# Loading the key and value weights inside the retention, and attention's tables inside the projection, in a one-core Trainium2 decoder layer

## The chip, the core and the metric

The kernel is one launch on one core of a Trainium2 chip. The metric is the device time of that launch in microseconds (us), the median of several executions. The engines are TensorE (PE in the rows; PEld is its weight load), VectorE (DVE), ScalarE (ACT), GpSimd (POOL) and SyncE (SP), which here only issues DMAs. Each engine works through its own queue in order. They meet in semaphores, and at the end of each block of the program in a barrier of all five.

## What is computed

One layer of a decoder trunk on 1088 tokens (1024 of a prompt, 64 of eight sampled sequences), width 1024, in float32. A feed-forward half step and a norm stand ahead of a mixer, and one more of each behind it. The change touches only the mixer:

```python
rq, rk, rv, rg, sq, sk, sv = project_in(x, w_in)        # retention q, k, v, gate; attention q, k, v
o_ret = retention(rq, rk, rv, state)                    # 8 heads x 64, chunks of 128 tokens
y_ret = silu(rg) * (o_ret - mean) * rsqrt(var + eps) * gn_w     # per head: the group norm
o_swa = sliding_window_attention(sq, sk, sv, bias, sinks)       # 8 query heads, 2 key/value heads
merged = concat([y_ret, o_swa]);  m = merged @ w_out
```

## The kernel before

A float32 product is made of three passes (L108): each operand is split into a rounded high part and a low part, and high x high, high x low, low x high are added up in PSUM. For weights the split is a ScalarE copy (`round_tile`, raw to `w_hi`) and a GpSimd subtraction (`split_tile`, raw minus `w_hi` to `w_lo`), and only then can TensorE use the tile.

**The order of the stages.** One block holds the first feed-forward step, the retention's projection and the retention (L1988 on). Two more blocks follow, one for the group norm with attention's projection, one for attention (L2043 to L2048); then a block for the output projection and the second feed-forward step.

**The end of the retention.** `retention_stage` goes through nine token tiles (eight of 128, the last of 64 sampled tokens). After the last one TensorE makes four more products for the sampled sequences' states (L1183), with two PSUM banks. VectorE folds each into `state_dec` (L1229), and when the fourth is folded SyncE issues the store of `state_dec` (L1089). The two stores of the prompt's state (L1087) were issued earlier. `outputs_stored` counts all three stores.

**Group norm and projection.** `group_norm_and_projection_stage` has six weight tiles (first keys and values, then four of queries) and three chunks of tokens for each, so 18 steps j of `project` (24 matmuls each, bank by bank). The group norm's nine token tiles u run between them. TensorE turns a tile of retention output to rows (`turn`, L1302); VectorE centres it (`centre`, L1352 to L1356); ScalarE squares it (L1403); VectorE sums the squares (L1362), ScalarE takes the root (`deviation`, L1408), VectorE the reciprocal (L1364, together `invert`); GpSimd multiplies (`normalise`, L1449); TensorE turns it back (`back`, L1312); VectorE multiplies by gain and gate (`gate`, L1373); ScalarE rounds this to `mix_hi` (`high`, L1421); GpSimd subtracts for `mix_lo` (`low`, L1455). TensorE's order is turn(0), turn(1), then for every j: project(j), turn(j+2), back(j-1). VectorE's is, for every u: centre(u), invert(u-1), gate(u-2). `gate` writes one of two `mixed` buffers, so from the third tile on it waits for `low` of the tile two before it (`lo_done`). ScalarE and GpSimd follow the loops of L1426 and L1463. The two slots of `stage` take the raw weights; SyncE waits for `room`, the three stores of the retention, ahead of its first load (L1290).

**Attention.** SyncE issues the two halves of the bias table, the sampled tokens' bias, the key and value caches and eight tiles of `w_out`, then the stores (L1557 on). TensorE makes scores for a block of 128 queries as a pair of key/value heads (`score_pair`, L1603, two pairs of score banks, of which the second pair is requested only after the first has been read: `biased`); VectorE scales them and adds the bias (L1675), which needs the scores and the table.

Of the kernel before, what the change touches and what calls it, by code (L numbers as in the profile page):

```python
# [63 lines left out]
class Stage:  # L64
# [5 lines left out]
    def __init__(self, sync=None, scalar=None, gpsimd=None, tensor=None, vector=None, sync_early=None,  # L70
# [5 lines left out]
                 added=None, sync_second=None):  # L76
# [9 lines left out]
        self.added, self.sync_second = added, sync_second  # L86

# [943 lines left out]
def retention_stage(core, at, tables_at, tables_room, ready, tables, g_chunk, g_dec, state_in, q_t, k_t, k_tok, v_tok, state_out,  # L1031
# [21 lines left out]
    q_dec = [m.put(f"{tag}q_dec{i}", [P, PAIRS, P]) for i in range(2)]  # L1053
    probs = [m.put(f"{tag}probs{i}", [P, 2, PAIRS * P]) for i in range(2)]
# [20 lines left out]
    def sync(sp):  # L1075
# [170 lines left out]
    return Stage(sync=sync, gpsimd=gpsimd, tensor=tensor, vector=vector, scalar=scalar, outputs_stored=(stored, 48))  # L1246


def group_norm_and_projection_stage(core, at, at_small, eps, gn_w, o_t, gate_t, mix_hi, mix_lo, w_in, xh, xl, ident,
                                    q_t, k_t, v_tok, room):  # L1250
# [13 lines left out]
    mixed = [m.put(f"{tag}mixed{u}", [P, PAIRS, P]) for u in range(2)]  # L1264
    m = Layout(core.nc, at)
    rows = [m.put(f"{tag}rows{u}", [P, HEADS, HD]) for u in range(3)]
    squares = m.put(tag + "squares", [P, HEADS, HD])
    stats = [m.put(f"{tag}stats{u}", [P, 5, HEADS]) for u in range(3)]
    w_hi = [m.put(f"{tag}w_hi{n}", [P, D_MODEL], F32R) for n in range(2)]
    w_lo = [m.put(f"{tag}w_lo{n}", [P, D_MODEL], F32R) for n in range(2)]  # L1270
# [17 lines left out]

    def sync(sp):
# [100 lines left out]

    def scalar(act):
        def round_tile(n):
            act.wait_ge(staged[n % 2], 16 * (n // 2) + 16)
            if n >= 2:
                act.wait_ge(proj_done, N * (n - 1))
            act.activation(w_hi[n % 2][:, :], stage[:, n % 2, :], ACT.Copy).then_inc(w_hi_done, 1)

# [20 lines left out]
        def high(u):  # L1418
            a, b = tile_tokens(u)
            act.wait_ge(gated, u + 1)  # L1420
# [822 lines left out]
```

## Time and profile before

| | us |
|---|---|
| median of 3 runs | 2205.27 |
| lowest, highest | 2204.52, 2205.83 |
| the profiled execution | 2202.61 |
| its span in the trace | 2200.8 |

| stretch of the profiled span | from, to (us) |
|---|---|
| end of the retention's block, group norm with projection | about 1052 to 1171 |
| attention | about 1171 to 1262 |
| everything ahead and behind | 0 to 1052, 1262 to 2201 |

All times in the rows count from the start of the span. A row of a timeline merges equal instructions that follow each other: the first number is the start of the first, the second the time from there to the end of the last. What stands in square brackets is how long the engine had been idle before it and who ended the wait. PEclk is the clock that TensorE was granted, as a share of 2.4 GHz.

### The profile page before, as it was taken

What the parts mean: (1) busy time and instruction counts of PE and PEld (TensorE: products, weight loads), DVE (VectorE), ACT (ScalarE), POOL (GpSimd) and SP (SyncE); (2) the same over time, 40 slices, a digit from 0 to 9 for tenths busy, and PEclk for the clock granted to TensorE, in tenths of its full rate; (3) what the DMA queues carried; (4) which work ended last, traced back from release to release, by engine and by line L of the source; (5) the groups of instructions that cost most, each with busy time, mean ns of one, the idle gap of its engine ahead of it and who ended that gap; (6) DMA issues with size and microseconds to landing.
All of it is one profiled execution on the core that took longest, in us unless ns stands there. A gap on an engine that the chain in (4) does not pass through costs nothing. (4 is left out here: it accounts for less than half of the span.)

```text
span 2200.8 us, 31129 instructions
## 1 busy us (share of the span) xinstructions
PE 2111.7 (96%) x11989; PEld 1937.3 (88%) x11989; DVE 910.0 (41%) x1690; ACT 507.0 (23%) x887; POOL 518.4 (24%) x257
## 2 busy tenths in 40 slices
PE   8999999999999989999786799899999999999997
PEld 8999999999999979998685478899999999999996
DVE  5534343443534360004434823434434343535346
ACT  4121211111111252111134722311111111121215
POOL 4221212122121231223142412221221212121213
PEclk9999999999999999999798999999999999999999
DMA  7111010101011021101104030101010101111012
GB/s 279 35 52 57 29 57 29 57 29 57 29 57 47 30 91 42 46 29 42 60 20 144 1 120 1 58 29 58 29 57 29 57 29 57 40 46 57 29 58 82
DMA packets 38058, 118.40 MB, mean 54 GB/s; under 512 B 6255, under 2 KB 10863, under 8 KB 37743
## 3 DMA queue, kind: packets, MB, share of 16 engines
q1 hardware_dynamic: 37999, 117.58, 15.0%
q8 instruction: 41, 0.67, 0.1%
q14 instruction: 18, 0.15, 0.0%
HBM read 106.29 MB, written 11.27 MB: 53 GB/s over the span
## 5 line engine op out<-in xcount | busy, mean ns | idle before, releaser
L111 PE MATMUL bank<-x_hi,f_w_hi 128*128 128x362 f32 (+1 forms) x2104 | 688.8, 327 | 7.5 <-issue 5.6
L113 PE MATMUL bank<-x_hi,f_w_low 128*128 128x362 f32 (+1 forms) x2104 | 690.3, 328 | 0.0
L355 POOL TENSOR_TENSOR f_w_low<-f_w_raw,f_w_hi 128x1024 fp32r<-128x1024 f32 x132 | 317.3, 2420 | 1179.3 <-ACT f_w_hi L285 1179.3
L543 DVE TENSOR_TENSOR acc<-bank,acc 128x512 f32<-128x512 f32 x720 | 467.1, 688 | 8.2 <-PE bank L441 5.8
L521 DVE TENSOR_TENSOR f_h_full<-bank,f_silu 128x362 f32<-128x362 f32 (+1 forms) x132 | 70.7, 535 | 818.2 <-PE bank L113 815.9
L111 PEld LDWEIGHTS bank<-x_hi,f_w_hi 128*128 128x128 f32 x2104 | 396.7, 189 | 9.6 <-issue 7.8
L113 PEld LDWEIGHTS bank<-x_hi,f_w_low 128*128 128x128 f32 x2104 | 396.4, 188 | 0.0
L112 PE MATMUL bank<-x_lo,f_w_hi 128*128 128x362 f32 (+1 forms) x1056 | 345.8, 327 | 0.0
L112 PE MATMUL bank<-x_low,f_w_hi 128*128 128x362 f32 (+1 forms) x1048 | 342.9, 327 | 0.0
L439 PE MATMUL bank<-f_w_hi,f_h_hi 128*128 128x512 f32 x640 | 250.8, 392 | 0.0
L441 PE MATMUL bank<-f_w_low,f_h_hi 128*128 128x512 f32 x640 | 250.1, 391 | 0.0
L440 PE MATMUL bank<-f_w_hi,f_h_lo 128*128 128x512 f32 x640 | 249.9, 390 | 0.0
L294 ACT ACTIVATE f_silu<-bank 128x362 f32<-128x362 f32 (+1 forms) x132 | 62.5, 474 | 683.7 <-PE bank L113 683.7
L112 PEld LDWEIGHTS bank<-x_lo,f_w_hi 128*128 128x128 f32 x1056 | 199.2, 189 | 0.9
L112 PEld LDWEIGHTS bank<-x_low,f_w_hi 128*128 128x128 f32 x1048 | 197.2, 188 | 0.8
L300 ACT ACTIVATE f_h_hi<-f_h_full 128x362 fp32r<-128x362 f32 (+1 forms) x132 | 67.0, 508 | 529.0 <-DVE f_h_full L521 529.0
L441 PEld LDWEIGHTS bank<-f_w_low,f_h_hi 128*128 128x128 f32 x640 | 120.1, 188 | 26.7
L439 PEld LDWEIGHTS bank<-f_w_hi,f_h_hi 128*128 128x128 f32 x640 | 120.1, 188 | 25.0 <-issue 0.7
L440 PEld LDWEIGHTS bank<-f_w_hi,f_h_lo 128*128 128x128 f32 x640 | 120.1, 188 | 24.6
L285 ACT ACTIVATE f_w_hi<-f_w_raw 128x1024 fp32r<-128x1024 f32 x132 | 134.0, 1044 | 32.2 <-DMA f_w_raw<-ffn_in 32.2
L111 PE MATMUL bank<-x_hi,rp_w_hi 128*128 128x362 f32 (+1 forms) x384 | 127.1, 331 | 3.9 <-ACTq L903 3.9
L113 PE MATMUL bank<-x_hi,rp_w_low 128*128 128x362 f32 (+1 forms) x384 | 126.3, 329 | 0.0
(194 smaller groups left out, 2233.9 us busy)
## 6 DMA issues: line engine op xcount, KB each, us to landing
f_w_raw<-ffn_in SPq DMA_DIRECT2D x132, 512.0 KB, 4.4
rp_w_raw<-w_ret_in SPq DMA_DIRECT2D x16, 512.0 KB, 3.5
acc<-x_rows_in SPq DMA_DIRECT2D x2, 2048.0 KB, 11.2
kept_rows<-acc SPq DMA_DIRECT2D x8, 512.0 KB, 2.7
ow_raw<-w_out_in SPq DMA_DIRECT2D x8, 512.0 KB, 10.5
y_out<-acc SPq DMA_DIRECT2D x8, 512.0 KB, 2.7
n_rows<-ln_rows_in SPq DMA_DIRECT2D x6, 512.0 KB, 8.5
gp_stage<-w_att_in SPq DMA_DIRECT2D x6, 512.0 KB, 3.4
```

Of the source, the lines that this page charges most:

```text
L111: pe.matmul(out, wh, xh, start=first, stop=False)
L112: pe.matmul(out, wh, xl, start=False, stop=False)
L113: return pe.matmul(out, wl, xh, start=False, stop=last)
L285: act.activation(flat(w_hi[s][j]), flat(w_raw[s][j]), ACT.Copy).then_inc(down_hi if j == DOWN else gu_hi, 1)
L294: act.activation(silu[:, buffer_of(f, s, c), 0:b - a], gate_ps[pair_of(f, s, c)][:, 0:b - a], ACT.Silu).then_inc(silu_done, 1)
L300: act.activation(h_hi[s][:, a:b], h_full[:, buffer_of(f, s, c), 0:b - a], ACT.Copy).then_inc(h_hi_done, 1)
L355: pool.tensor_tensor(flat(w_lo[s][j]), flat(w_raw[s][j]), flat(w_hi[s][j]).bitcast(F32), ALU.subtract).then_inc(done, 1)
L439: pe.matmul(out, h_hi[s][:, u], hi, start=True, stop=False)
L440: pe.matmul(out, h_lo[s][:, u], hi, start=False, stop=False)
L441: pe.matmul(out, h_hi[s][:, u], lo, start=False, stop=True).then_inc(down_done, 1)
L521: dve.tensor_tensor(h_full[:, at, 0:b - a], up_ps[pair_of(f, s, c)][:, 0:b - a], silu[:, at, 0:b - a], ALU.mult).then_inc(pair_free, 1)
L543: dve.tensor_tensor(acc[:, t, d], down_ps[(n + 2 * s) % 4][:, :], acc[:, t, d], ALU.add).then_inc(down_free, 1)
```

## The change

Four things are moved; no arithmetic is added or taken away.

1. The raw key and value weights (tiles 0 and 1) get buffers of their own, `first`, over the retention's keys. SyncE loads them once the last scores have been made (`keys_read`), ahead of the store of `state_dec`, which becomes `sync_last`. Tile 0 is rounded and split in the retention's block (`scalar_early`, `gpsimd_early`), into the place of the retention's `probs` once its last output is made (`probs_read`). Tile 1 waits on ScalarE for `room`, since its buffers lie over `state`, which is still being stored.
2. Tiles 2 to 5 use the two slots of `stage`; tile 2 no longer follows tile 0 there, so the block issues four weight loads in place of six. The third `rows` buffer and `squares` get new places.
3. In the loops, ScalarE does `high` ahead of `evacuate` and `round_tile`, and GpSimd does `low` ahead of `split_tile`.
4. Attention's bias, tables and caches are issued in the projection's block, once the last gate is applied (`gated`), over the places of `ret_q` and `ret_gate`.

```diff
 def retention_stage(...)
+    def sync_last(sp):
         sp.wait_ge(dec_state_done, PAIRS)
         sp.dma_start(state_dec_out, state_dec[:, :, :, :]).then_inc(stored, 16)
...
+                 keys_read=(scored, 2 * (LAST + 1)), probs_read=(out_done, LAST + 1), end=probs_at)
 def group_norm_and_projection_stage(...)
+    m = Layout(core.nc, at_first)
+    first = [m.put(f"{tag}first{n}", [P, D_MODEL]) for n in range(2)]
...
+    def raw(n):
+        return first[n][:, :] if n < 2 else stage[:, n % 2, :]
+    def sync_early(sp):
+        sp.wait_ge(*keys_read)
+        for n in range(2):
+            sp.dma_start(raw(n), source(n)).then_inc(staged[n], 16)
     def sync(sp):
         sp.wait_ge(*room)
-        for n in range(TILES):
-            if n >= 2:
-                sp.wait_ge(w_lo_done, n - 1)
-            sp.dma_start(stage[:, n % 2, :], source(n)).then_inc(staged[n % 2], 16)
+        for n in range(2, TILES):
+            sp.wait_ge(w_lo_done, n - 1)
+            sp.dma_start(raw(n), source(n)).then_inc(staged[n % 2], 16)
...
+    def scalar_early(act):
+        act.wait_ge(*probs_read)
+        round_tile(act, 0)
...
         def high(u):
             act.wait_ge(gated, u + 1)
+            if u == 0:
+                act.wait_ge(w_lo_done, 2)
...
         square(0)
         deviation(0)
-        round_tile(0)
-        round_tile(1)
+        act.wait_ge(*room)
+        round_tile(act, 1)
         for j in range(STEPS):
             if j + 1 < TOKEN_TILES:
                 square(j + 1)
                 deviation(j + 1)
+            if 0 <= j - 2 < TOKEN_TILES:
+                high(j - 2)
             evacuate(j)
             if j % N == N - 1 and j // N + 2 < TILES:
-                round_tile(j // N + 2)
-            if 0 <= j - 2 < TOKEN_TILES:
-                high(j - 2)
+                round_tile(act, j // N + 2)
...
+    def gpsimd_early(pool):
+        split_tile(pool, 0)
...
-        split_tile(0)
         normalise(0)
-        split_tile(1)
+        split_tile(pool, 1)
         for j in range(STEPS):
             if j + 1 < TOKEN_TILES:
                 normalise(j + 1)
-            if j % N == N - 1 and j // N + 2 < TILES:
-                split_tile(j // N + 2)
             if 0 <= j - 2 < TOKEN_TILES:
                 low(j - 2)
+            if j % N == N - 1 and j // N + 2 < TILES:
+                split_tile(pool, j // N + 2)
 def attention_stage(...)
-    def sync(sp):
+    def sync_early(sp):
+        sp.wait_ge(*tables_room)
         for h in range(KVH):
             sp.dma_start(bias[:, h, :, :], tables["bias"][:, h, :, :]).then_inc(bias_in[h], 16)
         sp.dma_start(bias_dec[:, :, :, :], tables["bias_dec"]).then_inc(tables_in, 16)
         sp.dma_start(k_cache[:, :, :], caches["k"]).then_inc(dec_in, 16)
         sp.dma_start(v_cache[:, :, :], caches["v"]).then_inc(dec_in, 16)
+    def sync(sp):
         for k in range(KT):
             out_weights.load(sp, k)
 def decoder_layer(...)
             retention.sync(sp)
+            gp.sync_early(sp)
+            retention.sync_last(sp)
...
             retention.gpsimd(pool)
+            gp.gpsimd_early(pool)
...
             retention.scalar(act)
+            gp.scalar_early(act)
...
+            gp.sync(sp)
+            attention.sync_early(sp)
```

SyncE's queue before, from the retention's stores to the loads of attention (a branch ends and begins a block; `gp_stage` are the raw weights):

```order
L1087 DMA state_prompt_out<-rt_state_172 256x1x64 x2
L1089 DMA state_dec_out<-rt_state_dec 128x2048
L1989 UNCONDITIONAL_BRANCH
L1899 UNCONDITIONAL_BRANCH
L1294 DMA gp_stage<-w_att_in 128x1024 x6
L1898 UNCONDITIONAL_BRANCH
L1899 UNCONDITIONAL_BRANCH
L1559 DMA at_bias<-bias_in 128x1024 x2
L1560 DMA at_bias_dec<-bias_dec_in 128x768
L1561 DMA at_k_cache<-k_cache_in 128x1024
L1562 DMA at_v_cache<-v_cache_in 128x1024
L1486 DMA ow_raw<-w_out_in 128x1024 x8
```

and with the change:

```order
L1090 DMA state_prompt_out<-rt_state_172 256x1x64 x2
L1309 DMA gp_first_177<-w_att_in 128x1024
L1309 DMA gp_first_178<-w_att_in 128x1024
L1094 DMA state_dec_out<-rt_state_dec 128x2048
L2028 UNCONDITIONAL_BRANCH
L2088 UNCONDITIONAL_BRANCH
L1315 DMA gp_stage<-w_att_in 128x1024 x4
L1590 DMA at_bias<-bias_in 128x1024 x2
L1591 DMA at_bias_dec<-bias_dec_in 128x768
L1592 DMA at_k_cache<-k_cache_in 128x1024
L1593 DMA at_v_cache<-v_cache_in 128x1024
L2086 UNCONDITIONAL_BRANCH
```

The first two weight loads now stand ahead of the state's store and of the block's end, and the five loads of tables and caches ahead of the end of the projection's block.

GpSimd's queue before, from its last work in the retention to the projection's second weight tile:

```order
L1106 TENSOR_TENSOR rt_v_own<-ret_v_tok,rt_own 64x512
L1989 UNCONDITIONAL_BRANCH
L1903 UNCONDITIONAL_BRANCH
L1458 MEMSET att_v_tok 128x128
L1442 TENSOR_TENSOR gp_w_lo_4569<-gp_stage,gp_w_hi_4567 128x1024
L1449 TENSOR_TENSOR gp_rows_4560<-gp_rows_4560,gp_stats_4564 128x512
L1442 TENSOR_TENSOR gp_w_lo_4570<-gp_stage,gp_w_hi_4568 128x1024
```

and with the change:

```order
L1111 TENSOR_TENSOR rt_v_own<-ret_v_tok,rt_own 64x512
L1468 TENSOR_TENSOR gp_w_lo_185<-gp_first_177,gp_w_hi_184 128x1024
L2028 UNCONDITIONAL_BRANCH
L2096 UNCONDITIONAL_BRANCH
L1488 MEMSET att_v_tok 128x128
L1479 TENSOR_TENSOR gp_rows_179<-gp_rows_179,gp_stats_181 128x512
L1468 TENSOR_TENSOR gp_w_lo_187<-gp_first_178,gp_w_hi_186 128x1024
```

The split of tile 0 has moved ahead of the block's end, and the first normalisation now stands ahead of both other steps of the group norm's block.

GpSimd's queue in the group norm before, around the split of tile 2 (`gp_rows` is the normalisation, `mix_lo` the low part that `gate` waits for):

```order
L1449 TENSOR_TENSOR gp_rows_4560<-gp_rows_4560,gp_stats_4564 128x512
L1442 TENSOR_TENSOR gp_w_lo_4569<-gp_stage,gp_w_hi_4567 128x1024
L1455 TENSOR_TENSOR mix_lo<-gp_mixed_4558,mix_hi 128x4x128
L1449 TENSOR_TENSOR gp_rows_4561<-gp_rows_4561,gp_stats_4565 128x512
L1455 TENSOR_TENSOR mix_lo<-gp_mixed_4559,mix_hi 128x4x128
```

and with the change:

```order
L1479 TENSOR_TENSOR gp_rows_179<-gp_rows_179,gp_stats_181 128x512
L1485 TENSOR_TENSOR mix_lo<-gp_mixed_175,mix_hi 128x4x128
L1468 TENSOR_TENSOR gp_w_lo_185<-gp_stage,gp_w_hi_184 128x1024
L1479 TENSOR_TENSOR gp_rows_180<-gp_rows_180,gp_stats_182 128x512
L1485 TENSOR_TENSOR mix_lo<-gp_mixed_176,mix_hi 128x4x128
```

The low part and the split have changed places; the same is done at tiles 3 and 4.

## Rows read from the trace of the kernel before

**Rows 1.** The page, busy time: share of the span, instructions
```profile
PE 2111.7 (96%) x11989; PEld 1937.3 (88%) x11989; DVE 910.0 (41%) x1690; ACT 507.0 (23%) x887; POOL 518.4 (24%) x257
```

**Rows 2.** Stretches of TensorE: us, PE busy (count), PEclk, DMA share, GB/s
```profile
1057.00:1068.00 11.00, 11.00 (x88) 0.50 0.01 1
...
1080.00:1084.00 4.00, 4.00 (x13) 0.50 0.39 131
...
1132.00:1135.00 3.00, 3.00 (x12) 0.51 0.00 0
...
1177.00:1183.00 6.00, 4.83 (x20) 0.50 1.03 414
```

**Rows 3.** Timeline, retention to projection: start, us, engine, line, what [idle <-releaser]
```profile
1052.34 1.27 SPq L1087 DMA_DIRECT2D state_prompt_out<-rt_state  x2
...
1061.27 0.77 ACT L1243 ACTIVATE ret_q<-bank 64x256 f32<-64x256 f32 x2 [7.71 <-PE bank L1157]
...
1068.96 0.35 SPq L1089 DMA_DIRECT2D state_dec_out<-rt_state_dec  x1
...
1069.77 1.94 PE L1302 MATMUL bank<-small,ret_q 128*128 128x128 f32 x8 [1.64 <-PEq L1989]
...
1072.88 10.70 SPq L1294 DMA_DIRECT2D gp_stage<-w_att_in  x4
...
1076.42 1.06 ACT L1396 ACTIVATE gp_w_hi<-gp_stage 128x1024 fp32r<-128x1024 f32 x1 [1.44 <-DMA gp_stage<-w_att_in]
1077.55 2.34 POOL L1442 TENSOR_TENSOR gp_w_lo<-gp_stage,gp_w_hi 128x1024 fp32r<-128x1024 f32 x1 [7.62 <-ACT gp_w_hi L1396]
...
1079.95 0.67 PE L111 MATMUL bank<-x_hi,gp_w_hi 128*128 128x362 f32 x1 [8.24 <-POOL gp_w_lo L1442]
```

**Rows 4.** Timeline of VectorE and GpSimd in the group norm
```profile
1099.79 0.20 DVE L1364 RECIPROCAL gp_stats<-gp_stats 128x8 f32<-128x8 f32 x1 [0.37 <-ACT gp_stats L1408]
...
1101.13 2.41 POOL L1442 TENSOR_TENSOR gp_w_lo<-gp_stage,gp_w_hi 128x1024 fp32r<-128x1024 f32 x1
...
1108.51 0.20 DVE L1364 RECIPROCAL gp_stats<-gp_stats 128x8 f32<-128x8 f32 x1 [0.37 <-ACT gp_stats L1408]
...
1109.80 1.27 POOL L1455 TENSOR_TENSOR mix_lo<-gp_mixed,mix_hi 128x512 fp32r<-128x512 f32 x1
...
1111.17 1.13 DVE L1373 SCALAR_TENSOR_TENSOR gp_mixed<-bank,small,ret_gate 128x128 f32<-128x128 f32 x4 [2.46 <-POOL mix_lo L1455]
...
1114.79 0.20 DVE L1364 RECIPROCAL gp_stats<-gp_stats 128x8 f32<-128x8 f32 x1 [0.37 <-ACT gp_stats L1408]
...
1129.75 0.20 DVE L1364 RECIPROCAL gp_stats<-gp_stats 128x8 f32<-128x8 f32 x1 [0.37 <-ACT gp_stats L1408]
```

**Rows 5.** Timeline of TensorE in the projection: the transposes back
```profile
1122.45 0.66 PE L1312 MATMUL bank<-small,gp_rows 128*128 128x128 f32 x4 [1.62 <-POOL gp_rows L1449]
...
1131.13 0.66 PE L1312 MATMUL bank<-small,gp_rows 128*128 128x128 f32 x4 [4.01 <-POOL gp_rows L1449]
...
1137.24 0.46 PE L1312 MATMUL bank<-small,gp_rows 64*128 64x64 f32 x4
```

**Rows 6.** Timeline, start of attention, VectorE and TensorE
```profile
1171.46 1.16 PE L1603 MATMUL bank<-att_k,att_q 64*128 64x128 f32 x16 [0.81 <-PEq L1898]
...
1175.37 0.76 DVE L1675 SCALAR_TENSOR_TENSOR at_scores<-bank,at_bias 128x256 f32<-128x256 f32 x2 [23.25 <-DMA at_bias<-bias_in]
...
1178.03 3.79 PE L1603 MATMUL bank<-att_k,att_q 64*128 64x256 f32 x16 [5.41 <-DVE at_scores L1675]
...
1181.91 1.29 DVE L1675 SCALAR_TENSOR_TENSOR at_scores<-bank,at_bias 128x512 f32<-128x512 f32 x2 [2.41 <-PE bank L1603]
```

**Rows 7.** Timeline of TensorE later in attention
```profile
1209.79 1.23 PE L1624 MATMUL bank<-small,at_scores 128*128 128x128 f32 x8 [2.27 <-ACT at_turned L1752]
1210.95 3.47 PE L1603 MATMUL bank<-att_k,att_q 64*128 64x256 f32 x16
```

**Rows 8.** Line 1222: duration ns min/median/max, first and last start
```profile
L1222 DVE SCALAR_TENSOR_TENSOR rt_state<-rt_state,small,bank x56: 264/280/289, 1021.8 to 1052.0; 64x64 f32<-64x64 f32 x56
```

More of the change, by code:

```diff
@@ L86, in __init__ @@
         self.added, self.sync_second = added, sync_second
+        self.keys_read, self.probs_read, self.gated = keys_read, probs_read, gated
+        self.sync_last = sync_last
 class Layout:
@@ L1244, in scalar, with group_norm_and_projection_stage @@
                                    ACT.Copy)
-    return Stage(sync=sync, gpsimd=gpsimd, tensor=tensor, vector=vector, scalar=scalar, outputs_stored=(stored, 48))
-def group_norm_and_projection_stage(core, at, at_small, eps, gn_w, o_t, gate_t, mix_hi, mix_lo, w_in, xh, xl, ident,
-                                    q_t, k_t, v_tok, room):
+    return Stage(sync=sync, sync_last=sync_last, gpsimd=gpsimd, tensor=tensor, vector=vector, scalar=scalar,
+                 outputs_stored=(stored, 48),
+                 keys_read=(scored, 2 * (LAST + 1)), probs_read=(out_done, LAST + 1), end=probs_at)
+def group_norm_and_projection_stage(core, at, at_small, at_first, at_weights, eps, gn_w, o_t, gate_t, mix_hi, mix_lo, w_in,
+                                    xh, xl, ident, q_t, k_t, v_tok, keys_read, probs_read, room):
     tag = "gp_"
@@ L1264, in group_norm_and_projection_stage @@
     mixed = [m.put(f"{tag}mixed{u}", [P, PAIRS, P]) for u in range(2)]
+    m = Layout(core.nc, at_first)
+    first = [m.put(f"{tag}first{n}", [P, D_MODEL]) for n in range(2)]
     m = Layout(core.nc, at)
-    rows = [m.put(f"{tag}rows{u}", [P, HEADS, HD]) for u in range(3)]
+    rows = [m.put(f"{tag}rows{u}", [P, HEADS, HD]) for u in range(2)]
+    stats = [m.put(f"{tag}stats{u}", [P, 5, HEADS]) for u in range(3)]
+    assert m.at <= at_weights
+    m = Layout(core.nc, at_weights)
+    w_hi, w_lo = [], []
+    for n in range(2):
+        w_hi.append(m.put(f"{tag}w_hi{n}", [P, D_MODEL], F32R))
+        w_lo.append(m.put(f"{tag}w_lo{n}", [P, D_MODEL], F32R))
+    rows.append(m.put(tag + "rows2", [P, HEADS, HD]))
     squares = m.put(tag + "squares", [P, HEADS, HD])
-    stats = [m.put(f"{tag}stats{u}", [P, 5, HEADS]) for u in range(3)]
-    w_hi = [m.put(f"{tag}w_hi{n}", [P, D_MODEL], F32R) for n in range(2)]
-    w_lo = [m.put(f"{tag}w_lo{n}", [P, D_MODEL], F32R) for n in range(2)]
     SUM, NEG, SSQ, STD, INV = range(5)
@@ L1988, in decoder_layer @@
                                 o["state_prompt"], o["state_dec"])
+    gp = group_norm_and_projection_stage(
+        core, att_end, mix_lo_att_at, free, retention.end, eps, part("gn_w"), ret_q, ret_gate, mix_hi, mix_lo, i["w_att"],
+        xh, xl, ident, att_q, att_k, att_v_tok, retention.keys_read, retention.probs_read, retention.outputs_stored)
+    attention = attention_stage(core, att_end, mixer_at, i, gp.gated, part("sinks"), part("sinks_dec"),
+                                {"k": i["k_cache"], "v": i["v_cache"]}, att_q, att_k, att_v_tok, ident,
+                                mix_hi, mix_lo, o, out_weights)
     with nc.Block() as block:
@@ L2041, in _ @@
             retention.tensor(pe)
-    one_stage_block(nc, group_norm_and_projection_stage(
-        core, att_end, mix_lo_att_at, eps, part("gn_w"), ret_q, ret_gate,
-        mix_hi, mix_lo, i["w_att"], xh, xl, ident, att_q, att_k, att_v_tok, retention.outputs_stored))
-    one_stage_block(nc, attention_stage(core, att_end, mixer_at, i, part("sinks"), part("sinks_dec"),
-                                        {"k": i["k_cache"], "v": i["v_cache"]}, att_q, att_k, att_v_tok, ident,
-                                        mix_hi, mix_lo, o, out_weights))
+    with nc.Block() as block:
+        @block.sync
+        def _(sp):
+            gp.sync(sp)
+            attention.sync_early(sp)
+        block.tensor(gp.tensor)
+        block.vector(gp.vector)
+        block.scalar(gp.scalar)
+        block.gpsimd(gp.gpsimd)
+    one_stage_block(nc, attention)
     norm2 = Norm(core, "n2_", eps, acc, rows2, stats2, squares2, ident, core.psum[:, 3072:4096], xh2, xl2, rescale=2 * ALPHA)
```

33 lines of the change are left out of this document (18 added, 15 removed).

## The prediction

> **What bounds the kernel now.** First the page's busy times: TensorE is busy for 96% of the span [rows 1]. So the time is TensorE's work plus its idle stretches plus what its lower clock costs, and the change adds no TensorE work. I therefore looked for TensorE's idle time and for its granted clock in the stretch that is touched, from 1052 to about 1262 us. The reader is to see four places there.
>
> First place: TensorE ends its first two transposes at 1069.77 + 1.94 = 1071.71 and starts the projection at 1079.95, after 8.24 us idle, released by the split of weight tile 0 [rows 3]. The chain behind that reads backwards as split 2.34, rounding 1.06, landing of a load issued at 1072.88, and that load waited until the state's store of 1068.96 had landed [rows 3].
>
> Second place: inside the projection TensorE waits for a normalised tile on GpSimd, 1.62 us before 1122.45 and 4.01 us before 1131.13 [rows 5]. GpSimd is only the last link. VectorE's gate waits 2.46 us for the low part there [rows 4].
>
> Third place: directly behind the 4.01 us, the clock is at half (1.2 GHz) from 1132 to 1135 [rows 2].
>
> Fourth place: in attention VectorE waits until 1175.37 for the bias table, although the scores were there at 1171.46 + 1.16 = 1172.62; TensorE, which may not make the next scores until these are read, is idle for 5.41 us and then works at half clock [rows 2, 6].
>
> **Term 1, the early weights: 8.2 us.** In the new order SyncE issues both loads right behind the prompt state's stores, which end at 1052.34 + 1.27 = 1053.61. They need the last scores made, which holds by then, since the stored state is later in TensorE's order. A load of this size took 1076.42 - 1072.88 = 3.54 us from its issue to the rounding [rows 3], so both are in by about 1058. ScalarE is free for the rounding after its last output copies, 1061.27 + 0.77 = 1062.04, rounds until 1063.10, and GpSimd splits until 1065.45. The block lasts until the store issued at 1068.96, so 3.5 us of cover are left. If the cover were gone, each us would come back one for one. The store is now behind two issues on SyncE, but those are done 15 us earlier: nothing. So the projection can start at 1071.71 in place of 1079.95. What is late next is the transposes themselves, 1.94 us, which stay.
>
> Two things could take from this. The split now runs beside VectorE's fold of `state_dec`, on which TensorE waits. No row has this pair, but VectorE's same form with one operand in PSUM ran 264 to 289 ns, with GpSimd's multiplications beside it, over the whole retention [rows 8], so the nearest row says zero; if both folds that it can meet took double (0.75 us each, my bound from rows of VectorE's 128 x 512 forms such as the 1.29 us for two in rows 6), it would be 1.5 us. And ScalarE's wait for the stores ahead of tile 1 ends when SyncE's ended before, at 1072.88; ScalarE is then in the first square and root. Tile 1 is needed three steps later, after more than 12 us: nothing.
>
> **Term 2, the clock at the start: 0.5 us.** The clock was at half from 1057 on and through the first 4 us of the projection; by 1084.1 it had come back [rows 2]. That is 4.1 us after TensorE resumed. In the new order TensorE goes on without a break from 1069.77. If the clock returns 4.1 us after that, 1.9 us less of the projection passes at half clock, which gives 1.0 us; if the 4.1 us count from 1071.71, nothing. Against the first stands that it stayed at half for the 11 us before 1068, with TensorE busy all the time [rows 2]. I take the middle, 0.5, and keep 0 and 1.0 for the range.
>
> **Term 3, the order of ScalarE and GpSimd: 6.2 us.** I follow one turn of the loop from a reciprocal, at 1108.51: GpSimd normalises, then does the low part, 1109.80 + 1.27 = 1111.07; the gate starts at 1111.17, takes 1.13, then come the next centring and sum, and the next reciprocal is at 1114.79 [rows 4]. The turn is 6.28 us. TensorE needs less than that for a step, so this loop is what it waits for in the end. From 1099.79 to 1108.51 the turn is 8.72, since the split (1101.13, 2.41 us) stands between normalising and the low part. From 1099.79 to 1129.75 there are four turns in 29.96 us, two with a split; at 6.28 each they take 25.12. That gives 4.84 us, provided that the split fits behind the low part: there GpSimd is idle from 1111.07 to beyond 1114.79, 3.7 us, against 2.4 [rows 4]. The high part now stands ahead of evacuation and rounding, so it is ready when GpSimd has normalised. The rounding, 1.06 us, has the 1.27 us of the low part as cover. What the split releases is a weight tile three steps of TensorE away. The evacuations come later by one high part; with four PSUM banks TensorE needs them four steps on: nothing.
>
> The first reciprocals of the loop hang on TensorE and shift with term 1. So the transposes back of tile 7 come at 1131.13 - 8.24 - 4.84 = 1118.05. TensorE still waits there, about 2 us in place of 4, and I expect the clock to stay up, as after the 1.62 us [rows 5]. The step from 1131.13 to 1137.24 took 6.11 us, and about 3.2 us of it at half clock cost 1.6 [rows 2, 5]; without that it is 4.5. Tile 8 then becomes the one that is late: its turn has no centring and is 1.55 us shorter, 4.73, so about 0.2 us waits. Term 3 is 4.84 + 1.6 - 0.2 = 6.2. Its bounds are 0, if the loop doesn't shorten, and 6.5.
>
> **Term 4, attention's tables: 2.7 us, and 0.5 for the clock.** All gates are done around 1126 in the new order, 30 us before the projection ends, and five loads are quick to issue. Nothing is queued behind SyncE's wait but these loads and the block's end. The table is there, so VectorE starts when the scores are, at 1172.62 plus the 0.09 us that it took from 1178.03 + 3.79 to 1181.91 [rows 6]: 1175.37 - 1172.71 = 2.7 us. After that the same chain runs as before.
>
> TensorE's idle time there shrinks from 5.41 to about 2.7 us. The second pair of scores took 3.79 us at half clock; at full clock it would be 1.9, and VectorE's wait for it, 2.41 us, would nearly go. For a full gain speaks the 1.62 us above. Against it, later in attention idle stretches of 2.3 us and less led to 3.47 us for the same pair of scores [rows 7]. I take 0.5, nearer to the second, for it is the same work; the range has 0 to 1.9. The page "TensorE: Matmul & The Clock Gate" of the Trainium skill (section "What's actually happening") says that the gate falls after an idle stretch of the engine, judged by a monitor that runs free of the program. By it the shorter stretch would keep 2.4 GHz here more often than the later rows show, and the sum would be 1.4 us larger.
>
> Behind attention everything starts from a block's end and shifts along. What the clock does in the rest of attention may differ by 1 us either way.
>
> **The sum.** 8.2 + 0.5 + 6.2 + 2.7 + 0.5 = 18.1 us. The profiled execution of 2202.61 would be 2184.5; it lies 2.7 us under the median. From the median: 2205.27 - 18.1 = 2187.2.
>
> **Rivals.** (a) *The split still costs a turn.* If the rounding comes late (ScalarE first waits for a gate), GpSimd takes the split when the next reciprocal is due, and term 3 gives nothing: 18.1 - 6.2 = 11.9 us, 2193.4. For it speaks that ScalarE's order became stricter; against it the 3.7 us of idle time and that the gates are a turn ahead of their high parts. (b) *The clock returns early and stays up at both places:* terms 2 and 4 at their upper ends, 18.1 + 0.5 + 1.4 = 20.0 us, 2185.3. That is where the page's rule would lead. (c) *The early part is hidden:* contention with the folds (1.5), or a block start that takes longer with the new code, takes 2 to 4 us of term 1: about 2190. (d) *Slower: the clock does not return.* TensorE was busy for 11 us at half clock up to 1068 without release [rows 2]. If the projection, which now follows that work nearly without a break, also stayed at half, each us of its matmuls at full clock would take two. The gain is used up at 18 us of such work, of 72 us in all (18 steps of 4.0, the 4.5 above less the transposes): the worst case is 72 - 18 = 54 us slower, 2259. Against it: both times when projection matmuls ran at half clock [rows 2], at 1080 and at 1132, it was back within about 4 us. (e) *It doesn't do what it says,* because a wait orders the early loads behind the block after all: then term 1 is gone and 9.9 us remain, 2195.4. The semaphores named in the change allow no such order that I can see.
>
> **Chances.** The sum as it stands 0.58; (b) 0.17; (c) 0.11; (a) 0.09; (e) 0.03; (d) 0.02. The likeliest is the sum, 2187.2. The range takes in (b) with 1.5 us for the spread of the runs and the rest of attention, and on the other side (c) and most of (a): 2183.5 to 2193. A measurement of this kernel tells 0.2%, 4.4 us, from no change: faster by more 0.96, within it 0.02, slower 0.02.
>
> **What would show it.** Right for term 1: TensorE's first projection matmul directly behind the second transposes, with no idle time released by GpSimd; the split ended before the block does. Term 2: a granted clock back at full less than 6 us after the transposes start. Term 3: reciprocals 6.3 us apart with and without a split, a longest wait for a normalised tile of about 2 us, no half clock in the middle of the projection. Term 4: no wait of VectorE for a DMA, but one for TensorE's scores, and TensorE's first idle stretch in attention at 2.7 us. Wrong: turns of 8.7 us for tiles with a split (a), folds of `state_dec` longer than 0.75 us (c), or half clock beyond the first 6 us of the projection (d).

## The result, and the profile after

| | before | after |
|---|---|---|
| median of the runs taken together | 2205.55 | 2187.76 |
| lowest, highest | 2204.52, 2205.90 | 2183.72, 2191.25 |
| span of the profiled execution | 2200.8 | 2189.1 |

The ratio is 0.9919, with a 95% interval of 0.9902 to 0.9937: 17.8 us less, where 18.1 us were forecast. The profiled execution of the changed kernel is the slowest of its four (2191.25 us). The difference of the two spans is therefore only 11.7 us, and part of the work below is to say why.

The page of the changed kernel: the span, then each engine's busy time, share and instructions. TensorE's share has gone from 96% [rows 1] to 97%.

```profile
span 2189.1 us, 31133 instructions
PE 2116.2 (97%) x11989; PEld 1941.3 (89%) x11989; DVE 911.7 (42%) x1690; ACT 506.9 (23%) x887; POOL 518.3 (24%) x257
```

The end of the retention, the start of the projection (start, us, engine, line, what, in brackets the idle time before and its releaser), against [rows 3]:

```profile
1054.92 1.08 SPq L1309 DMA_DIRECT2D gp_first<-w_att_in  x2
...
1065.11 1.06 ACT L1416 ACTIVATE gp_w_hi<-gp_first 128x1024 fp32r<-128x1024 f32 x1
...
1066.24 2.35 POOL L1468 TENSOR_TENSOR gp_w_lo<-gp_first,gp_w_hi 128x1024 fp32r<-128x1024 f32 x1 [14.47 <-ACT gp_w_hi L1416]
...
1072.03 0.34 SPq L1094 DMA_DIRECT2D state_dec_out<-rt_state_dec  x1
...
1072.83 1.94 PE L1323 MATMUL bank<-small,ret_q 128*128 128x128 f32 x8 [1.63 <-PEq L2028]
...
1074.42 0.65 PE L113 MATMUL bank<-x_hi,gp_w_hi 128*128 128x362 f32 x1
```

The early loads go out at 1054.92, ScalarE rounds tile 0 until 1066.17, GpSimd has split it by 1068.59, and the block's last store is issued at 1072.03. The projection starts 1.59 us after the transposes did, with no idle time; it was 10.18 us. That is 8.59 us. VectorE's four folds of `state_dec`, two of which meet the split, take 0.75 us each, as in the kernel before. The whole end of the retention stands some 3 us later than before (the state's store at 1072.03, in place of 1068.96): 1.3 us of this were lost ahead of the stores at 1052, 1.8 behind them, both by TensorE's clock, see below.

Stretches of TensorE in the changed kernel, against [rows 2] (from:to, us, PE busy and count, PEclk, DMA share, GB/s):

```profile
1056.00:1068.00 12.00, 12.00 (x150) 0.50 0.28 90
1068.00:1073.00 5.00, 3.37 (x9) 0.50 0.06 25
1073.00:1076.00 3.00, 3.00 (x13) 0.50 0.75 309
1077.00:1080.00 3.00, 3.00 (x21) 1.00 0.47 171
1121.00:1124.00 3.00, 3.00 (x12) 0.50 0.00 0
1165.00:1168.00 3.00, 3.00 (x16) 0.50 0.98 381
```

The clock is at half until 1076 and back at full from 1077. So it returns about 1.7 us after the projection's start at 1074.42 (2.3 us in e4_after, the same kernel again), where it took 4.1 us before. It still falls in the middle of the projection (1121 to 1124) and after the first scores of attention (1165 to 1168).

VectorE and GpSimd in the group norm, against [rows 4]:

```profile
1093.28 0.20 DVE L1385 RECIPROCAL gp_stats<-gp_stats 128x8 f32<-128x8 f32 x1 [0.37 <-ACT gp_stats L1433]
...
1094.57 1.30 POOL L1485 TENSOR_TENSOR mix_lo<-gp_mixed,mix_hi 128x512 fp32r<-128x512 f32 x1
...
1095.82 2.40 POOL L1468 TENSOR_TENSOR gp_w_lo<-gp_stage,gp_w_hi 128x1024 fp32r<-128x1024 f32 x1
...
1097.72 0.53 DVE L1375 TENSOR_SCALAR gp_stats<-gp_stats 128x8 f32<-128x8 f32 x1
...
1099.94 0.20 DVE L1385 RECIPROCAL gp_stats<-gp_stats 128x8 f32<-128x8 f32 x1 [0.37 <-ACT gp_stats L1433]
...
1106.23 0.20 DVE L1385 RECIPROCAL gp_stats<-gp_stats 128x8 f32<-128x8 f32 x1 [0.37 <-ACT gp_stats L1433]
```

From one reciprocal to the next it is now 6.66 us with a split (1093.28 to 1099.94; 8.72 before) and 6.29 without one (1099.94 to 1106.23; 6.28 before). The split stands behind the low part, as meant. New is the length of the tiny TENSOR_SCALAR of L1375, 128 x 8 elements in SBUF: it takes 0.53 us in place of 0.17 and ends at 1098.25, just after the split's end at 1095.82 + 2.40 = 1098.22.

TensorE's transposes back, against [rows 5]:

```profile
1113.90 0.66 PE L1333 MATMUL bank<-small,gp_rows 128*128 128x128 f32 x4 [0.89 <-POOL gp_rows L1479]
...
1120.53 1.07 PE L1333 MATMUL bank<-small,gp_rows 128*128 128x128 f32 x4 [2.02 <-POOL gp_rows L1479]
...
1126.64 0.46 PE L1333 MATMUL bank<-small,gp_rows 64*128 64x64 f32 x4
```

The longest wait for a normalised tile has gone from 4.01 to 2.02 us. The step behind it still takes 1126.64 - 1120.53 = 6.11 us, exactly as before.

The start of attention, against [rows 6]:

```profile
1160.87 1.16 PE L1636 MATMUL bank<-att_k,att_q 64*128 64x128 f32 x16 [0.81 <-PEq L2086]
...
1162.11 0.76 DVE L1708 SCALAR_TENSOR_TENSOR at_scores<-bank,at_bias 128x256 f32<-128x256 f32 x2 [20.59 <-PE bank L1636]
...
1164.77 3.62 PE L1636 MATMUL bank<-att_k,att_q 64*128 64x256 f32 x16 [2.74 <-DVE at_scores L1708]
...
1168.49 1.29 DVE L1708 SCALAR_TENSOR_TENSOR at_scores<-bank,at_bias 128x512 f32<-128x512 f32 x2 [2.24 <-PE bank L1636]
```

VectorE now waits for TensorE's scores, no longer for a DMA, and starts 1.24 us after them in place of 3.91. TensorE's idle time is 2.74 us in place of 5.41. But the second pair of scores still takes 3.62 us (3.79 before), and VectorE waits 2.24 us for it (2.41).

### The profile page after: what moved, and what is told of

It reads as the page before. It is cut to its first block and busy times, and to the rows that moved or that the text cites. A ratio compares the mean times of both kernels' runs of the same rounds, so it can differ in the third digit from the quotient of the medians.

```text
span 2189.1 us, 31133 instructions
## 1 busy us (share of the span) xinstructions
PE 2116.2 (97%) x11989; PEld 1941.3 (89%) x11989; DVE 911.7 (42%) x1690; ACT 506.9 (23%) x887; POOL 518.3 (24%) x257
```

## The experiments

Each was timed beside the kernel before on the same chip; "of before" is the difference from that median. Kernels whose results stand in one table were timed together, with the same runs of the kernel before. The diffs are against the changed kernel, unless said otherwise.

### One part at a time

**e1_weights** is the changed kernel with both loops in the old order and the tables loaded in attention again:

```diff
-            if 0 <= j - 2 < TOKEN_TILES:
-                high(j - 2)
             evacuate(j)
             if j % N == N - 1 and j // N + 2 < TILES:
                 round_tile(act, j // N + 2)
+            if 0 <= j - 2 < TOKEN_TILES:
+                high(j - 2)
...
-            if 0 <= j - 2 < TOKEN_TILES:
-                low(j - 2)
             if j % N == N - 1 and j // N + 2 < TILES:
                 split_tile(pool, j // N + 2)
+            if 0 <= j - 2 < TOKEN_TILES:
+                low(j - 2)
...
-            attention.sync_early(sp)
```

> Only the early weights (and the early split of tile 0) of the change; loops and table loads in the old order. Theory, the terms stand apart and add up: 8.2 us faster than before plus 0 to 1.2 for the clock that returns sooner, so 8.2 to 9.4, with the group norm's turns still 6.28 and 8.7 us and TensorE's 4 us wait still there. Rival, the terms hide each other: with the projection earlier the group norm's chain becomes the limit at once and less than 6 us is left.

**e2_order** is the kernel before with nothing but the two loops in the new order:

```diff
+            if 0 <= j - 2 < TOKEN_TILES:
+                high(j - 2)
             evacuate(j)
...
-            if 0 <= j - 2 < TOKEN_TILES:
-                high(j - 2)
...
+            if 0 <= j - 2 < TOKEN_TILES:
+                low(j - 2)
             if j % N == N - 1 and j // N + 2 < TILES:
                 split_tile(j // N + 2)
-            if 0 <= j - 2 < TOKEN_TILES:
-                low(j - 2)
```

> Only the new order of ScalarE and GpSimd in the two loops. Theory: two turns of the group norm's loop lose the split, less the 0.35 us that the profile of the changed kernel shows left in them: 4.1 us faster. If TensorE's granted clock also stays at full behind the last wait, 1.6 more, 5.7 us. Rival: the low part wasn't what the gate waited for, and the turns with a split stay at 8.7: 0 to 1 us.

**e3_tables** keeps the early tables alone; weights and loops are as before:

```diff
-            gp.sync_early(sp)
             retention.sync_last(sp)
...
-            gp.gpsimd_early(pool)
...
-            gp.scalar_early(act)
```

> Only attention's tables and caches issued in the projection's block. Theory: VectorE starts 2.7 us sooner in attention, and the time falls by 2.7 us, up to 1.5 us more or less by where TensorE's clock falls in attention. Rival: another wait of attention takes the place and the end of attention moves by under 1 us.

**e4_after** is the changed kernel once more.

> The changed kernel once more, for a second profile and five more times. The profile on record was its slowest run. Theory, the spread of this kernel is TensorE's granted clock at a few places (end of the retention, the last wait of the group norm, attention): the profiled stretches differ there and nowhere else, and the times lie between 2183 and 2192. Rival, the spread comes from the DMAs or from the parts that weren't touched: the stretches differ ahead of 1050 us or behind attention.

| | median us | of before (2204.88) | ratio, 95% |
|---|---|---|---|
| e1_weights | 2195.73 | -9.15 | 0.9964 [0.9950, 0.9977] |
| e2_order | 2200.17 | -4.71 | 0.9979 [0.9970, 0.9988] |
| e3_tables | 2202.33 | -2.55 | 0.9991 [0.9982, 1.0000] |
| e4_after | 2188.55 | -16.33 | 0.9931 [0.9918, 0.9945] |

The three single gains add up to 16.41 us, the whole kernel gives 16.33: nothing speaks for parts that lean on each other, though each gain has an interval of 2 to 3 us to either side. The tables alone reach the edge of what can be told from no change; in the trace VectorE's start moves by 2.66 us. In this set of runs the whole gain is 16.3 us and not the 17.8 of the result; both intervals hold either value.

e1_weights, TensorE at the start of the projection, and its last wait for a normalised tile:

```profile
1070.42 1.94 PE L1323 MATMUL bank<-small,ret_q 128*128 128x128 f32 x8 [1.63 <-PEq L2029]
...
1072.01 0.65 PE L113 MATMUL bank<-x_hi,gp_w_hi 128*128 128x362 f32 x1
...
1122.16 1.11 PE L1333 MATMUL bank<-small,gp_rows 128*128 128x128 f32 x4 [4.10 <-POOL gp_rows L1479]
```

The projection starts 1.59 us after the transposes do, as in the changed kernel. So the whole of that effect is due to the early weights. The wait of about 4 us is still there with the old loops.

e2_order, VectorE's reciprocals and TensorE's last wait:

```profile
1102.27 0.20 DVE L1364 RECIPROCAL gp_stats<-gp_stats 128x8 f32<-128x8 f32 x1 [0.37 <-ACT gp_stats L1408]
...
1108.93 0.20 DVE L1364 RECIPROCAL gp_stats<-gp_stats 128x8 f32<-128x8 f32 x1 [0.37 <-ACT gp_stats L1408]
...
1129.52 0.66 PE L1312 MATMUL bank<-small,gp_rows 128*128 128x128 f32 x4 [1.97 <-POOL gp_rows L1449]
```

6.66 us from one to the other with a split, and a wait of 1.97 us: the loop order alone makes the shorter turns. Behind this wait the clock is at half from 1131 to 1134.

e3_tables, the first scores and the first use of the table:

```profile
1171.92 1.16 PE L1636 MATMUL bank<-att_k,att_q 64*128 64x128 f32 x16 [0.82 <-PEq L2083]
...
1173.17 0.76 DVE L1708 SCALAR_TENSOR_TENSOR at_scores<-bank,at_bias 128x256 f32<-128x256 f32 x2 [20.61 <-PE bank L1636]
```

VectorE starts 1.25 us after the scores, released by TensorE: this effect is the tables' alone.

### Where the rest of a turn goes

Turns with a split should have fallen to 6.28 us and stood at 6.66, and the last wait was still 2 us long. Two theories on the 0.37 us: VectorE's small TENSOR_SCALAR is held up by the split, or ScalarE's rounding of the next weight tile, which stands between two norm steps, makes `deviation` late. And one on the whole: the loop from `gate` to `low` and back to `gate` is what sets the turn, since only two `mixed` buffers are there.

**e5_mixed3** has a third `mixed` buffer, over a dead part of the retention's storage, so `gate` waits for `low` of the tile three before it:

```diff
+    mixed.append(Layout(core.nc, at_first - 4 * PAIRS * P).put(tag + "mixed2", [P, PAIRS, P]))
...
-            if u >= 2:
-                dve.wait_ge(lo_done, u - 1)
+            if u >= 3:
+                dve.wait_ge(lo_done, u - 2)
...
-            act.activation(mix_hi[:, 0:PAIRS, a:b], mixed[u % 2][:, :, 0:b - a], ACT.Copy).then_inc(hi_done, 1)
+            act.activation(mix_hi[:, 0:PAIRS, a:b], mixed[u % 3][:, :, 0:b - a], ACT.Copy).then_inc(hi_done, 1)
```

> The changed kernel with a third buffer for the gated tile (2 KB that are free between the gate and the feed-forward part), so that the gate waits for the low part of three tiles before, not two. Theory, the loop reciprocal, normalise, low part, gate, centring is what TensorE waits for: the gate's waits for the low part go, the turns become TensorE's own 4.9 us, both waits of TensorE for a normalised tile (0.9 and 2.0 us) go, and with them the clock's fall at the end of the group norm (1.6 us): 4.5 us faster than the changed kernel. Rival, GpSimd or VectorE are the limit by their work: turns stay above 6 us and less than 1 us is gained.

**e6_round** moves ScalarE's rounding of a weight tile behind the next step's square, away from `high` and `evacuate`:

```diff
                 square(j + 1)
+                if j:
+                    next_round(j - 1)
                 deviation(j + 1)
...
             evacuate(j)
-            if j % N == N - 1 and j // N + 2 < TILES:
-                round_tile(act, j // N + 2)
+            if j + 1 >= TOKEN_TILES:
+                next_round(j)
```

> The changed kernel with ScalarE's rounding of a weight tile moved behind the next step's square. In the changed kernel turns with a split take 6.65 us, not 6.28. Theory P: VectorE's small subtraction of the mean's table (TENSOR_SCALAR, 128x8, 0.53 in place of 0.17 us) waits for GpSimd's split beside it, so this edit changes nothing: 6.65 stays, same time. Theory A: the rounding delays the square, and VectorE with it: turns of 6.28, 0.7 us faster.

**e8_pool_only** puts ScalarE's loop back into its old order and leaves GpSimd's new:

```diff
-            if 0 <= j - 2 < TOKEN_TILES:
-                high(j - 2)
             evacuate(j)
             if j % N == N - 1 and j // N + 2 < TILES:
                 round_tile(act, j // N + 2)
+            if 0 <= j - 2 < TOKEN_TILES:
+                high(j - 2)
```

> The changed kernel with ScalarE's loop in the old order (evacuate and round ahead of the high part) and GpSimd's in the new. Theory: in a turn with a rounding the high part ends 1.5 us later, 0.6 us after GpSimd asks for it, so two turns are 0.6 us longer and the rest as in the changed kernel: about 1 us slower than it. Rival: ScalarE's order is worth nothing, or all of the gain is ScalarE's (turns of 8.7 us come back).

**e9_fused** takes the TENSOR_SCALAR away: one instruction multiplies the sum by -1/64 and adds it to the tile, with the tile in PSUM as its other operand:

```diff
-            dve.tensor_scalar(st[0:w, NEG, :], st[0:w, SUM, :], -1.0 / HD, None, ALU.mult).then_inc(averaged, 1)
-            dve.wait_ge(averaged, 2 * u + 2)
-            dve.tensor_tensor(rows[u % 3][0:w, :, :], x, st[0:w, NEG, :].unsqueeze(2).to_broadcast([w, HEADS, HD]),
-                              ALU.add).then_inc(centred, 1)
+            dve.scalar_tensor_tensor(rows[u % 3][0:w, :, :], st[0:w, SUM, :].unsqueeze(2).to_broadcast([w, HEADS, HD]),
+                                     -1.0 / HD, x, ALU.mult, ALU.add).then_inc(centred, 1)
```

> The changed kernel with the centring fused: one instruction of VectorE adds the sum times -1/64 to the tile in PSUM, and the small TENSOR_SCALAR between is gone. Theory P (the small instruction waits for GpSimd's split): all turns become 6.07 us (6.28 less 0.21), with or without a split, 1.5 us over the four turns; TensorE's last wait is then under 1.5 us, and if the clock stays up, 1.6 us more. Theory A (ScalarE's rounding delays the square): turns of 6.07 without and about 6.4 with a split.

| | median us | of before (2204.94) | ratio, 95% | turns | projection to scores | last wait |
|---|---|---|---|---|---|---|
| e5_mixed3 | 2182.30 | -22.64 | 0.9897 [0.9882, 0.9912] | 6.66, 4.29, 4.28, 4.29 | 81.53 | none |
| e6_round | 2189.67 | -15.27 | 0.9927 [0.9913, 0.9940] | 6.66, 6.30, 6.28, 6.64 | 86.50 | 2.04 |
| e8_pool_only | 2189.38 | -15.56 | 0.9927 [0.9914, 0.9941] | 7.23, 6.30, 6.28, 7.22 | 86.10 | 2.60 |
| e9_fused | 2185.64 | -19.30 | 0.9910 [0.9895, 0.9925] | 6.10, 6.10, 6.08, 6.08 | 83.16 | 1.40 |

Turns are from reciprocal to reciprocal; the first and the fourth have a split (they are 6.66, 6.30, 6.28, 6.64 in e4_after, with 86.60 us from the first projection matmul to the first scores).

e6_round, ScalarE's rounding, then VectorE:

```profile
1093.17 1.05 ACT L1416 ACTIVATE gp_w_hi<-gp_stage 128x1024 fp32r<-128x1024 f32 x1
...
1096.35 0.53 DVE L1375 TENSOR_SCALAR gp_stats<-gp_stats 128x8 f32<-128x8 f32 x1
...
1098.56 0.20 DVE L1385 RECIPROCAL gp_stats<-gp_stats 128x8 f32<-128x8 f32 x1 [0.37 <-ACT gp_stats L1433]
```

The rounding is elsewhere, and nothing has changed: TENSOR_SCALAR is still 0.53 us long, the turn still 6.66. The theory of the rounding falls.

e9_fused, VectorE's one centring beside the split, its reciprocals, and TensorE's last wait:

```profile
1094.91 0.69 DVE L1375 SCALAR_TENSOR_TENSOR gp_rows<-gp_stats,bank 128x512 f32<-128x512 f32 x1
...
1096.56 0.20 DVE L1383 RECIPROCAL gp_stats<-gp_stats 128x8 f32<-128x8 f32 x1 [0.37 <-ACT gp_stats L1431]
...
1102.66 0.20 DVE L1383 RECIPROCAL gp_stats<-gp_stats 128x8 f32<-128x8 f32 x1 [0.37 <-ACT gp_stats L1431]
...
1116.20 0.66 PE L1333 MATMUL bank<-small,gp_rows 128*128 128x128 f32 x4 [1.40 <-POOL gp_rows L1477]
```

With an operand in PSUM, the centring beside the split takes 0.69 us, as long as without a split beside it. Turns with and without a split are equal (6.08 to 6.10), and with that the theory of the held-up TENSOR_SCALAR stands: 0.37 us of a turn with a split are the overlap, 0.20 us of every turn are the instruction itself.

e5_mixed3, GpSimd's split and VectorE's TENSOR_SCALAR inside it, the same pair beside GpSimd's low part, and TensorE's transpose back, now without a wait:

```profile
1092.96 2.39 POOL L1469 TENSOR_TENSOR gp_w_lo<-gp_stage,gp_w_hi 128x1024 fp32r<-128x1024 f32 x1
...
1093.39 1.99 DVE L1376 TENSOR_SCALAR gp_stats<-gp_stats 128x8 f32<-128x8 f32 x1
...
1098.35 1.29 POOL L1486 TENSOR_TENSOR mix_lo<-gp_mixed,mix_hi 128x512 fp32r<-128x512 f32 x1
...
1098.91 0.77 DVE L1376 TENSOR_SCALAR gp_stats<-gp_stats 128x8 f32<-128x8 f32 x1
...
1114.40 0.60 PE L1334 MATMUL bank<-small,gp_rows 128*128 128x128 f32 x4
```

Here the small instruction starts 0.43 us after the split did and lasts 1.99 us, until the split ends (1095.35 against 1095.38). The low part holds it up as well: 0.77 us, to 1099.68, where the low part ends at 1099.64. It no longer matters: the other turns are 4.28 us, less than a TensorE step of 4.5, and no wait for a normalised tile is left. From the projection's first matmul to the first scores it is 81.53 us, against 18 steps x 4.5 = 81. This stretch is now bound by TensorE alone. So the loop over the two `mixed` buffers was what bounded it in the changed kernel. For the kernel before, where no run has a third buffer, the gate's wait of 2.46 us for the low part [rows 4] says the same, but it isn't tested.

e8_pool_only, GpSimd's low part, which waits for the high part, and TensorE's last wait; then stretches of TensorE around it (columns as above):

```profile
1093.66 1.30 POOL L1485 TENSOR_TENSOR mix_lo<-gp_mixed,mix_hi 128x512 fp32r<-128x512 f32 x1 [0.54 <-ACT mix_hi L1448]
...
1120.20 0.66 PE L1333 MATMUL bank<-small,gp_rows 128*128 128x128 f32 x4 [2.60 <-POOL gp_rows L1479]
```

```profile
1116.00:1120.00 4.00, 1.59 (x10) 1.00 0.41 125
1120.00:1123.00 3.00, 2.80 (x18) 1.00 0.02 8
```

With the old ScalarE order a turn with a split is 0.57 us longer: GpSimd waits 0.54 us for the high part. That is what ScalarE's half of the reordering is worth to the loop; the rest of the fall from 8.72 us is GpSimd's, and neither rival holds. The 1 us more that was expected doesn't show in the time, which is that of e6_round in the same table (2189.38 and 2189.67). In the profiled runs that is the clock: it didn't fall here behind the wait of 2.60 us, and the step behind it took 4.74 us in place of 6.11.

### Is anything left in the loop?

**e10_both** has both edits, the third `mixed` buffer and the fused centring.

> The changed kernel with the third buffer for the gated tile and the fused centring. With the third buffer alone VectorE's small TENSOR_SCALAR took up to 1.99 us beside GpSimd's split, 5.8 us over its last five tiles, but no wait of TensorE was left in the projection. Theory, TensorE is then the limit of this stage: the fused centring shortens VectorE's turns and the time stays that of the third buffer alone within 0.5 us. Rival, VectorE's delay still reached TensorE through the banks: 1 us or more faster.

**e11_mixed3_again** is e5_mixed3 once more.

> The changed kernel with the third buffer alone, again, on the same chip as the fused one beside it. Theory: 2182.3 within its spread, with no wait of TensorE for a normalised tile and no low clock in the projection after its start.

| | median us | of before (2202.82) | ratio, 95% |
|---|---|---|---|
| e10_both | 2183.00 | -19.82 | 0.9905 [0.9889, 0.9922] |
| e11_mixed3_again | 2182.77 | -20.05 | 0.9909 [0.9893, 0.9926] |

The two can't be told apart (82.04 and 81.49 us from projection to scores, no waits in either). The 5.8 us named in the expectation are a miscount of mine: of the last five TENSOR_SCALARs in e5_mixed3 four are held up, one by a split (1.99 us) and three by a low part (0.77, 0.76 and 0.32), 3.84 us in all. They are off the path there. The third buffer is the best version of this study: 22.6 and 20.1 us less than before in its two timings, and by the medians 2182.3 and 2182.8 against 2187.8 and 2188.6 some 5 to 6 us less than the changed kernel (from different sets of runs, so this last difference has no interval).

## Where the profiled execution of the changed kernel lost its 4 us

e4_after is the same kernel, with a span of 2184.8 in place of 2189.1 us. The 4.3 us are 1.15 ahead of the stores at 1052, 1.67 from there to the store of `state_dec`, 1.48 in attention and nothing above 0.2 elsewhere. Two stretches of the changed kernel's first profile show the clock:

```profile
814.00:817.00 3.00, 3.00 (x12) 0.53 1.02 408
```

```profile
1054.00:1056.00 2.00, 0.71 (x12) 0.94 0.28 65
1056.00:1058.00 2.00, 2.00 (x38) 0.50 0.93 251
```

and the same stretches of e4_after:

```profile
814.00:817.00 3.00, 3.00 (x22) 0.92 1.02 416
```

```profile
1054.00:1056.00 2.00, 1.67 (x44) 1.00 0.64 126
1056.00:1058.00 2.00, 2.00 (x48) 0.70 0.98 365
```

At 814 to 817 the first has 0.53 of the clock, the second 0.92. At 1056 to 1058 it is 0.50 and 0.70. These two rows don't hold the same work, since the first profile is 1.15 us later here: TensorE resumes at 1055.48 in it and at 1054.33 in e4_after, and it has full clock for another 0.3 us in the one and about 2.5 us in the other. e4_after was expected to differ at the end of the retention, at the last wait and in attention; it differs at the first and the third, and at one place ahead of 1050 that only the rival had named, though there too it is the clock. The change touches nothing ahead of 1052, and the single-part kernels show both forms too: e2_order has the late form (1053.47 at the prompt state's stores, 18.43 us from there to the state's), e1_weights and e3_tables the early one (1052.59 and 17.03, 1052.58 and 16.98). The two halves of the late form also come apart: e6_round and e8_pool_only are at the prompt state's stores at 1052.24 and 1052.17 and yet take 18.38 and 18.50 us from there. So it is the run, not the kernel. That the whole spread of the changed kernel's times, 2183.7 to 2191.3, comes from such places is likely, but two profiles don't show it.

## Why the prediction was right, and where it was not

The forecast was 2187.2, the result 2187.76. By e4_after, whose execution resembles that of before, the spans differ by 16.0 us: 8.58 from the transposes to the projection, 4.91 from there to the scores, 2.67 to VectorE's start, 0.45 in attention, less 0.24 and 0.37 elsewhere.

**Term 1, the early weights: 8.2, measured 8.6** (e1_weights, with term 2: 9.15). Its steps held one by one. The cover was 1072.03 - 1068.59 = 3.4 us where 3.5 were named, and the folds beside the split cost nothing, so the lower of the two bounds was right. The measured 8.6 are the 8.24 us of idle time and 0.35 by which the first projection matmul overlaps the end of the transposes. Rivals (c), that contention hides part of it, and (e), that it isn't done, fall.

**Term 2, the clock at the start: 0.5, measured 1.2 and, in e4_after, 0.95.** The first projection step takes 4.87 us (1074.42 to 1079.29), 5.08 in e4_after, and 6.03 before. The clock was back 1.7 and 2.3 us after the projection's start, 3.4 and 3.9 us after the transposes' start: about my first reading, that the 4.1 us count from where TensorE resumes, with 1.0 us as its price. The middle was the wrong choice, and 1.0 was no upper bound.

**Term 3, the order of the loops: 6.2, measured 3.9 to 4.7** (3.9 is the 5.06 us from projection to scores less term 2's 1.16; 4.7 is e2_order by its medians; in its trace the stretch is 4.45 us shorter, 0.37 of them in the first step by the clock, which leaves 4.1). This is the term that failed, in two steps. First, "at 6.28 each they take 25.12": four turns take 25.87, since a turn with a split is 6.65. I checked only that the split fits behind the low part, not what VectorE does while it runs; e9_fused shows that it is the TENSOR_SCALAR. The page "SBUF — State Buffer" of the Trainium skill (section "Who interferes with whom") says that GpSimd shares a pair of SBUF ports with VectorE, that the one which begins first has the pair for its whole instruction, and that a `tensor_scalar` can be of the kind that needs it, while an instruction with at most one input in SBUF and outside the two-port modes does not. The traces agree: the TENSOR_SCALAR ends with the split, at 1098.25 and 1098.22, and the centring and the folds, with an operand in PSUM, keep their 0.69 and 0.75 us. So does a reciprocal of the same size with its one input in SBUF: 0.20 us at 1109.93 in e5_mixed3, inside a split from 1108.18 to 1110.58. Second, "I expect the clock to stay up, as after the 1.62 us", worth 1.6 us: the wait was 2.02 us as forecast, but the clock fell (0.50 from 1121 to 1124) and the step took 6.11 us again. The nearest row of before was a wait 0.4 us shorter, which I took for the same. With 4.1 us for the turns (29.96 - 25.87), nothing for the clock and the 0.2 taken off, the term is the 3.9 that were measured. Rival (a), that a split still stands in the way of the next normalisation, falls: a turn with one is 6.66 us, not 8.7.

**Term 4, the tables: 2.7, measured 2.67,** and 2.55 by the medians of e3_tables alone. **Its clock: 0.5, measured 0.2 and, in e4_after, 0.5.** The row of later attention was the better guide: 2.74 us of idle time, then half clock, 3.62 us for the pair. That 2.74 us occur in all nine profiles with the early tables, and the pair behind them takes 3.32 us in e4_after and 3.49 to 3.79 in the others, so the clock never stayed up there. The rule of the Trainium skill's page "TensorE: Matmul & The Clock Gate" (section "What's actually happening") had spoken for full clock more often behind the shorter stretch; these rows don't bear that out.

**The sum.** Term 2 was 0.5 to 0.7 too small and term 1 0.4, term 3 was 1.5 to 2.3 too large, term 4's clock by 0.3 at most. Errors of opposite sign partly cancelled. The three parts measured alone give 16.4 us and the repeat 16.3; against these 18.1 was 1.7 too much, and part of the closeness of 2187.2 to 2187.76 is the luck of four runs. The range from 2183.5 to 2193.0 holds both medians of the changed kernel. Rival (b), the clock back early and up at both places, was right on its first half alone. Rival (d), slower because the clock doesn't return, fell in every profile.

## What to carry to other kernels

When work is moved off a loop that paces an engine, follow the whole loop again with the moved piece in its new place: what runs beside it now, and which buffer closes the loop. Here one more buffer (e5_mixed3) gave another 5 to 6 us on top of the reordering of two engines, and with it the fused instruction gained nothing; whether the buffer would have given the whole without the reordering, no run tried. Don't put the clock behind a wait of about 2 us into a sum as a certainty: here it fell behind 1.97 to 2.04 us and stayed up behind 2.60, so it belongs in the range. And take a second profile before a difference of 4 us in 2200 is explained.

## What the runs showed of the hardware

A VectorE TENSOR_SCALAR of 128 x 8 elements from SBUF to SBUF, 0.17 us by itself, lasts until a GpSimd subtraction that began before it is over. Beside the split of a weight tile it takes 0.53, 0.54 and, off the path, 1.11 us in the changed kernel, and 1.99 us in e5_mixed3; beside the low part, up to 0.77 us in e5_mixed3. The VectorE instructions beside the same subtractions that have an operand in PSUM keep their time (0.69 and 0.75 us), and so do a reciprocal of 128 x 8 (0.20 us) and a sum over 128 x 512 (0.67 us) that read one operand from SBUF, both in e5_mixed3.

The length of TensorE's wait alone does not decide whether its clock falls behind it. Last waits of 1.97 (e2_order), 2.02 (the changed kernel) and 2.04 us (e4_after, e6_round) were each followed by about 3 us at half clock, as were those of 4.01 (before), 4.10 (e1_weights) and 4.08 (e3_tables). Behind 2.60 us (e8_pool_only), 1.62 (before) and 1.40 (e9_fused) it stayed up. What tells the 2.60 from the 1.97 stays open; no run here tried it.

Toward the end of the retention TensorE was busy without a gap for 12 us (1056 to 1068 in the changed kernel, 150 matmuls, most of them 64x64 against 64x8) and stayed at half clock; it was back at full 3.4 us after the transposes' start (3.9 in e4_after), once these and the projection's 128x128 against 128x362 followed. Why it stayed at half before stays open: no run changed that work alone.
